# Three expert weight units loaded as one transfer of 112 partitions and four of four partitions

## The reference, cut to what matters

```python
def swiglu(h, wg, wu, wd):
    return (jax.nn.silu(h @ wg) * (h @ wu)) @ wd

def moe_swiglu(h, router, wg, wu, wd):
    logits = (h @ router).astype(jnp.float32)
    top_v, top_i = lax.top_k(logits, TOP_K)          # TOP_K = 2
    top_w = jax.nn.softmax(top_v, axis=-1)
    comb = ...                                       # weight of each expert for each token
    out = jnp.zeros(h.shape, jnp.float32)
    for e in range(N_EXPERTS):                       # 8 experts
        out = out + comb[..., e:e + 1] * swiglu(h, wg[e], wu[e], wd[e])
    return out
```

## Time and profile before

| | |
|---|---|
| median of three runs | 1656.93 us |
| the profiled execution | 1656.72 us |
| its span, from the first instruction to the last | 1654.8 us |
| PE busy | 1624.8 us (98%) |
| DVE, ACT, POOL busy | 704.9, 447.9, 169.6 us |
| moved by DMA | 486.36 MB, 294 GB/s over the span |
| unit loads (line 793) | 160 of 2048 KB and 16 of 1024 KB |

### The profile page before, as it was taken

One profiled execution on the slowest core, in us unless ns is written; L12 is line 12 of the kernel. 1 busy time (PEld: TensorE's weight loads), 2 busy tenths in 40 slices (PEclk: granted clock), 3 DMA queues, 4 the chain that ended last, 5 costly groups with the idle time before them and its releaser, 6 DMA issues.

```text
span 1654.8 us, 31886 instructions
## 1 busy us (share of the span) xinstructions
PE 1624.8 (98%) x14156; PEld 955.2 (58%) x14156; DVE 704.9 (43%) x1188; ACT 447.9 (27%) x673; POOL 169.6 (10%) x166
## 2 busy tenths in 40 slices
PE   9999999999999999999999999999999899999997
PEld 8877677688888877776754335332343223433334
DVE  6669767655555669758541111211103011021121
ACT  6477423454344467523410000000000000000001
POOL 1264102200000075100400000000000000000000
PEclk9999999999999999999999999999999999999999
DMA  9743213655445743213999999999999999999995
GB/s 352 238 150 140 82 73 116 214 203 187 171 176 195 235 171 122 103 53 128 367 396 429 430 430 405 411 429 431 428 429 430 430 429 431 429 430 427 409 430 219
DMA packets 82463, 486.36 MB, mean 294 GB/s; under 512 B 5136, under 2 KB 11924, under 8 KB 58392
## 3 DMA queue, kind: packets, MB, share of 16 engines
q1 hardware_dynamic: 78272, 475.54, 71.5%
q0 software_dynamic: 1376, 5.05, 0.8%
q10 hardware_dynamic: 2680, 3.74, 0.7%
HBM read 479.54 MB, written 1.05 MB: 290 GB/s over the span
## 4 chain that ended last, share of the span: by engine, by line
PE 90%; DMA 5%; DVE 3%; ACT 3%; issue 0%; DVEq 0%; SPq 0%; ACTq 0%
PE bank L1492 29%; PE bank L2224 29%; PE bank L2246 12%; DMA slot<-moe_units_dram 4%; PE bank L1740 4%; PE bank L1482 2%; PE bank L1715 2%; PE bank L2179 1%; PE bank L2129 1%; PE bank L1513 1%; PE bank L2158 1%; PE bank L1774 1%; PE bank L1523 0%; PE bank L1665 0%; PE bank L1620 0%; DVE ring_lo L2295 0%
## 5 line engine op out<-in xcount | busy, mean ns | idle before, releaser
L2224 PE MATMUL bank<-slot,xg 128*32 128x512 f32 (+1 forms) x5120 | 491.4, 540 | 3.2 <-DMA slot<-moe_units_dram 3.0
L2224 PEld LDWEIGHTS bank<-slot,xg 128*32 128x32 f32 x5120 | 163.8, 110 | 305.8 <-issue 278.6
L2246 PE MATMUL bank<-slot,ehT 128*32 128x512 f32 (+1 forms) x2912 | 246.4, 494 | 8.0 <-DMA slot<-moe_units_dram 6.8
L2246 PEld LDWEIGHTS bank<-slot,ehT 128*32 128x32 f32 x2912 | 92.7, 110 | 153.0 <-issue 109.1
L1392 ACT ACTIVATE esg<-bank 128x512 f32<-128x512 f32 (+3 forms) x32 | 20.4, 637 | 496.0 <-PE bank L2224 496.0
L2295 DVE TENSOR_TENSOR ehm<-bank,esg 128x512 f32<-128x512 f32 (+3 forms) x32 | 23.7, 741 | 209.3 <-ACT esg L1392 209.3
L3085 DVE COPY ehT<-bank 128x512 f32<-128x512 f32 (+3 forms) x32 | 23.7, 741 | 192.9 <-PE bank L2179 192.9
L2295 DVE TENSOR_TENSOR ring_lo<-ring,i_hi 128x2048 fp32r<-128x2048 f32 (+2 forms) x36 | 80.5, 2240 | 58.1 <-ACT i_hi L1043 58.1
L2295 DVE TENSOR_TENSOR ring_lo<-ring,f_hi 128x2048 fp32r<-128x2048 f32 (+1 forms) x36 | 75.4, 2111 | 63.0 <-ACT f_hi L1317 63.0
L1492 PE MATMUL bank<-i_hi,ix_hi 128*128 128x512 f32 (+1 forms) x240 | 92.3, 385 | 0.0
L1492 PE MATMUL bank<-i_hi,ix_lo 128*128 128x512 f32 (+1 forms) x240 | 92.2, 384 | 0.0
(11 more groups left out here) (498 smaller groups left out, 2321.0 us busy)
## 6 DMA issues: line engine op xcount, KB each, us to landing
slot<-moe_units_dram SPq DMA_DIRECT2D x160, 2048.0 KB, 24.2
ring<-w_in_dram SPq DMA_DIRECT2D x25, 2048.0 KB, 8.0
slot<-moe_units_dram SPq DMA_DIRECT2D x16, 1024.0 KB, 7.9
ring<-w_branch_dram SPq DMA_DIRECT2D x6, 2048.0 KB, 7.8
ring<-ffn_w_gate_dram SPq DMA_DIRECT2D x5, 2048.0 KB, 7.8
ring<-ffn_w_up_dram SPq DMA_DIRECT2D x5, 2048.0 KB, 8.0
ring<-ffn_w_down_dram SPq DMA_DIRECT2D x5, 2048.0 KB, 7.6
ring<-w_o_dram SPq DMA_DIRECT2D x2, 2048.0 KB, 9.1
```

Source lines behind the costliest of these rows:

```text
L2224: ins = M(psum[GROUP * p:GROUP * p + GROUP, to:to + width], xg[:, x, o:o + GROUP], w[:, c, p, :], start=x == 0 and to % 512 == 0, stop=x = ...
L2246: ins = M(psum[to:to + GROUP, o:o + n], ehT[:, x, GROUP * i:GROUP * i + GROUP], w[:, c, c0:c0 + n], start=x == 0, stop=x == 27, skip_group ...
```

## The change

Units 4, 10 and 16 of the second item (`where == FIRST` in `item_units`) no longer come as one DMA of 128 partitions. Rows 0 to 111 come as one DMA on the semaphore that the unit had. Rows 112 to 127 come as four DMAs of four rows each, which share a semaphore of their own for each of the three units. PE waits for both semaphores before the first half of such a unit. Nothing else differs; the bytes and their places are the same.

```diff
+UNEVEN = (4, 10, 16)
+EVEN_ROWS = 112
...
+        self.uneven_loaded = {u: new(f"uneven_loaded{u}") for u in UNEVEN}
...
+                elif where == FIRST and u in UNEVEN:
+                    slot = slots[slot_of(where, UNITS * j + u)]
+                    src = moe_units[bass.ds(e, 1), u:u + 1].rearrange("o q (p n) -> p (o q n)", p=P)
+                    sp.dma_start(slot[0:EVEN_ROWS, :], src[0:EVEN_ROWS, :])\
+                        .then_inc(unit_loaded[slot_of(where, UNITS * j + u)], 16)
+                    for r in range(EVEN_ROWS, P, 4):
+                        sp.dma_start(slot[r:r + 4, :], src[r:r + 4, :]).then_inc(s.uneven_loaded[u], 16)
                 else:
                     unit(bass.ds(e, 1), j, u, where)
...
                     elif q % 2 == 0 or halves:
                         pe.wait_ge(unit_loaded[slot_of(where, u)], pair * (16 * again) + 16 * (loads + 1))
+                        if first and j and q // 2 in UNEVEN:
+                            pe.wait_ge(s.uneven_loaded[q // 2], 16 * ((P - EVEN_ROWS) // 4))
```

## The result

The changed kernel takes 1683.73 us (median of four runs, 1680.28 to 1685.34) against 1657.47 us for the kernel before in the same runs: 1.0164 times as long, interval 1.0151 to 1.0176; by the medians it is 26.3 us more. The profiled execution is the shortest of the four, 1680.28 us, with a span of 1678.5 us; 23.7 us more than that of before.

The account below looks back on a forecast made before the run. PE's matmuls bound it, the end set by a load landing at 1330.4. Three units cost 26.4 us; less a 2.4 lead, 4.3 and 0 to 3.2 given back, 18 us remain: 1674.7 us, range 1655 to 1685.

Parts of the forecast that it names:

- What bounds the kernel: Expert stage: PE's matmuls, with the end set by the load issued at 1290.9 landing at 1330.4, delay passed on us for us.
- Instructions at no cost: SP's extra issues, 1.3 us a unit, are hidden behind its waits, and PE's three more waits cost nothing: 0 for both.
- The price of the transfers: Units 4, 10, 16: 5.6 us for 112 rows plus 2.0 for each four-row transfer, 8.8 us more a unit, 26.4 in all.
- the prediction's second sum of 23 us: The same sum by the Trainium skill's figure, some 2.4 us for a four-row transfer: some 23 us in place of 18.
- Four engines late, twelve not: Small transfers fall on the same four engines; at own rate over three units, four have 5.5 us more, twelve 1.8 less.
- The give-back: After unit 16, the short queue before 1044 returns 4.3 us, later delays 0 to 3.2, leaving 17 to 20 at 1330.
- The lead of 2.4 us: The four engines may be ahead of the slowest engine before the changed units; 2.4 us taken off, bounds 0 and 5.
- The signs announced: Rate below 400 GB/s around 930, 960, 990; next units some 8 us later; PE gaps near 1013 and from 1060; shorter SP waits.
- Every engine at its own rate: Rival: the four engines come 3.1 us late at most and the gap eats it; no change, 1655.5 to 1658; 22%.
- Half the price: Rival: buffers hide half of the narrow transfers' slowness, 4.2 us more a unit; 3 to 6 us slower, 1661; 12%.
- Faster: Rival: the slowest engine up to 1330 is one of the twelve, with less work; up to 4.2 us gained, 1652.5; 8%.
- P1: Follow-up theory: how much of the 128 partitions a transfer spans at one time counts; even and odd 64: 1656 to 1661.

Follow-up runs that it names:

- the third place: Changed kernel with low halves of all 128 rows, eight four-row transfers of high halves at partitions 0 to 15 and 32 to 47, rest left out; 1656.83 us.

## Why the prediction came out as it did

The forecast was 18 us slower, with a range of its own up to 27 us; measured are 26.3. The path is as forecast, and the two prices that were added up are not.

**What bounds the kernel.** Right. The end is again set by the landing of a load of the expert stage, and PE has no new gap before 1006. The delay was carried by the DMA engines for more than 300 us, from 1020 to 1353, and reached the end us for us (23.3 at that landing, 23.7 in the span).

**Instructions at no cost.** Right. A small transfer's issue takes SP 253 to 308 ns, and SP has its cover; the run with two transfers of 128 partitions has a second issue and PE's added wait, and its time doesn't change; nor does that of the kernel with eight small transfers at the third place.

**The price of the transfers.** This is the step that failed in its sizes, and its two terms failed in opposite ways. "5.6 us for 112 rows" is 10.3 us by the rate of the first unit in the run with the 112 rows alone. By the medians of that run, and with 6.9 us given back as worked out from the run with one unit, it is (13.2 + 6.9) / 3 = 6.7 us above a whole unit's 4.88, 11.6 us on the slowest engine. "2.0 us for a four-row transfer" is too much: by the medians all four together add 26.3 - 13.2 = 13.1 us in three units, 4.4 us a unit, 1.1 us each beside the 112 rows, and by the work lost in the two profiled executions 4.9 us, 0.4 us each. The forecast of 8.8 us more for a unit (its terms make 8.7) had 0.7 of it from the 112 rows and 8.0 from the small ones; measured are 11.0, with 6.7 or more from the 112 rows and 4.4 or less from the small ones. That the sum came out near is luck to this extent, and a reader should not take it for a proof of the parts. The same goes for the prediction's second sum of 23 us: it lies nearer, but with 2.4 us for a small transfer it has more of the wrong term. Beside it the prediction had both copies of the earlier trace rows agree with the Trainium skill's count of ports. By that count only the copy of 15 partitions should be slow, as it reaches four ports, and not the one of 112, which reaches all 16. A likely source of the error, which no run tests: the earlier trace rows show one rate for the sum of a weight load and a copy, and I put all of the missing rate down to the copy alone, with the 112-row copy only 1.3 times as long as by its bytes.

**Four engines late, twelve not.** In part. Behind unit 16 the slowest engine is 30.9 us late, while the rate, a mean over all 16, has lost 26.7 us, 4.2 us less; with one 16-row transfer the two are 21.6 and 20.8 us (299, 425, 296, 378 and 303 GB/s in the five stretches, and a landing at 985.6 + 42.8). That is what an uneven share would do, and so are the 5.5 us between the medians of the two kernels, but it is argued: no view shows the engines one by one. The 20.8 us that remain with an even share show no favoured twelve: in the slow spells the rate falls to about half while the share stays at 1.00, more than four engines can lose.

**The give-back.** Right in size. Behind unit 16 the loads are 30.9 us late and the one that sets the end is 23.3 us late: 7.6 us are given back, at the upper end of 4.3 + (0 to 3.2). The runs with one unit and three make it 6.9 us. The lead of 2.4 us, which the prediction took off besides, no view can show. Of the 7.6 us, 3.6 can be seen as work, in the queue's short spell of before (416 GB/s from 1020 to 1040 against 374, 430 from 1040 to 1060 against 396). The other 4 us are about what the slowest engine was behind the mean, which suggests, and does not show, that it caught up with the others.

**The signs announced.** The rate fell at the three places named. PE's first gap for a load ended at 1010.64, where 1013 was forecast, but it was unit 15, a whole one, that PE waited for. The row of gaps, announced from about 1060 on, began some 30 us later: PE waited 0.70 us for a load before 1091.22. The units behind 4, 10 and 16 landed 6.4, 11.0 and 13.5 us later each time, not some 8. The small transfers of unit 16 landed 4.6 us behind its 112 rows, so the sign of being wrong (within 3 us) did not come. SP's waits were to be shorter and were not: from 840 to 1060 they are 192.2 us in 42 waits (195.6 in 45 before), from 1060 to 1340 241.7 us in 56 (239.7 in 56 before). SP goes on waiting for PE, which the late loads have made late too.

**The rivals.** "Every engine at its own rate" needs a rate of 430 throughout; it had 287 to 221. Yet it is what happens when the rows are well placed: the eight small transfers at 0 to 15 and 32 to 47. "Half the price" gave 4.2 us a unit, measured are 11.0. "Faster" needed a gain from less work on the slow engines; the runs that leave out an eighth or a half of the three units and keep the rate (7/8 of the columns, the middle 64) gained nothing (0.9997 and 1.0000), so there was none to be had, and no run points to a version faster than the kernel before.

**What stays open.** How the rows of a 112-row transfer are dealt out to the engines, and which engine meets which at what place, is in none of the views. That a transfer of 112 partitions is dear, and not its bytes or the number of transfers, is shown. That the place of the rows decides is shown for the 64-row and the small transfers; that the 112 rows are slow for the same reason is argued by likeness and not shown, and no run moved those 112 rows elsewhere. Nor does one rule cover all that was seen: P1 has the 64-row runs right, but of the small transfers that are spread alike, over four blocks of four, those at one place lose 2.4 us a unit and those at the other nothing.

## What to carry to other kernels

Where a stage lives on the DMA rate, cut a transfer by columns rather than by rows: here 128 partitions with 7/8 of the columns cost nothing, while 112 partitions with all columns, the same bytes, cost 13.2 us in three units by the medians, and 9.6 to 25.6 us from one execution to another. If rows have to be cut, look at the DMA rate of the stretch before the time, since a share of 1.00 with half the GB/s tells of slow transfers that the time may hide. And a sum that comes out right may hold two wrong terms: an experiment for each term is worth more than one for the sum.

## What the runs showed of the hardware that I had not expected

The slow spell takes more than the engines of the small transfers with it. I had expected slow transfers to hold up the engines that carry them; 227 GB/s against 428 from 924 to 938 at the same share are 201 missing, and a quarter of the engines has 107 to lose. With the 112 rows alone the rate falls as well (301 GB/s from 920 to 940).

TensorE's clock fell after the waits near 1010 and 1020. In the stretches of the kernel after (columns of the earlier trace rows), first the idle one, then those behind it:

```profile
1006.00:1010.00 4.00, 0.73 (x12) 0.16 (x4) 0.00 (x0) 0.00 (x0) 0.00 (x0) 1.00 1.03 233
1011.00:1013.00 2.00, 2.00 (x20) 0.74 (x16) 0.00 (x0) 0.00 (x0) 0.00 (x0) 0.50 0.94 197
...
1016.00:1018.00 2.00, 2.00 (x25) 0.78 (x28) 1.37 (x4) 0.00 (x0) 0.00 (x0) 1.00 0.86 188
...
1026.00:1028.00 2.00, 2.00 (x16) 0.63 (x12) 0.00 (x0) 0.00 (x0) 0.00 (x0) 0.50 1.05 451
1028.00:1030.00 2.00, 2.00 (x32) 0.86 (x27) 0.00 (x0) 0.00 (x0) 0.00 (x0) 0.99 1.05 442
```

PE waits for 3.9 us, then works at 0.50 of its clock, 1.2 GHz, and the 32 matmuls at 1010.64 take 4.48 us; the 32 at 1016.04, at 1.00 again, take 2.72. After the second wait, of 4.64 us, the same comes again. In the kernel before, waits of at most 1.3 us each leave it at 1.00, from 1320 to 1340 for one. It costs 1.8 us here and some more at 1024, and none of it should reach the end, as DMA moves 428 GB/s or more in every stretch of 20 us from 1040 to 1360 and PE is held by loads again from 1091 on.
